# Changing the order of two jobs on VectorE and of one on ScalarE in the steady steps of a two-layer trunk

## The reference

```python
# layer 0: stick-breaking
logits = einsum(q, k) * scale
log_keep = where(strict, log_sigmoid(logits) - logits, 0)
between = cumsum(log_keep, reverse=True) - log_keep
weights = where(strict, exp(log_sigmoid(logits) + between), 0);  out = weights @ v
# layer 1: differential
probs = softmax(q @ k * scale + alibi_bias)          # two maps
weights = probs[0] - lam * probs[1];                 out = rms_norm(weights @ v) * (1 - lam_init)
# both
y = (out * silu(z)) @ w_out;   x = x + gate * rms_norm(y)
```

## Time and profile before

| | |
|---|---|
| median of 3 runs | 1470.96 us (1470.79 to 1471.69) |
| the profiled execution | 1471.86 us, its span 1470.1 us |
| TensorE busy, share of the span | 94% |
| VectorE, ScalarE, GpSimd | 69%, 62%, 22% |
| mean granted clock of TensorE | 0.980 |
| stretch 115 to 640 us, steady stick pairs | TensorE 506.2 of 525 us, VectorE 434.1 (83%), ScalarE 336.2, GpSimd 149.3, granted clock 1.00 |
| stretch 640 to 745 us, last stick pair | TensorE 90.4 of 105 us, granted clock 0.93 |
| stretch 860 to 1330 us, steady differential pairs | TensorE 454.7 of 470 us, VectorE 279.2, ScalarE 326.4, GpSimd 105.8, granted clock 1.00 |
| one steady stick pair | 77.3 us (its 1024-wide scans begin at 269.65 and 347.00) |
| scans L1586 | 128, mean 1.37 us |

### The profile page before, as it was taken

How to read it: one execution, slowest core, us unless ns; L and a number is a source line. 1 busy time by engine, 2 the same in 40 slices (tenths; PEclk the granted TensorE clock), 3 DMA queues, 4 the chain that set the end, 5 groups by cost and what they waited for, 6 DMA issues and landing times. The chain is left out here.

```text
span 1470.1 us, 23466 instructions
## 1 busy us (share of the span) xinstructions
PE 1374.6 (94%) x7206; PEld 1131.8 (77%) x7206; DVE 1015.2 (69%) x1866; ACT 909.6 (62%) x1780; POOL 326.7 (22%) x255
## 2 busy tenths in 40 slices
PE   6889999999999999988999899999999999998987
PEld 3568878787878787876778678787878778786876
DVE  4557878887888787888578665656564656565654
ACT  3556656666666665676356566767576767676632
POOL 2002323232323232322100013222222212126000
PEclk8989999999999999998999999999999999999999
DMA  9111212020212121241043111001100010003113
GB/s 342 50 36 51 65 44 72 21 86 29 71 43 71 36 71 43 64 136 37 15 160 128 29 29 30 29 29 28 43 29 29 29 29 29 29 29 115 43 65 136
DMA packets 88591, 89.90 MB, mean 61 GB/s; under 512 B 3065, under 2 KB 68834, under 8 KB 88546
## 3 DMA queue, kind: packets, MB, share of 16 engines
q1 hardware_dynamic: 88256, 89.15, 19.2%
q10 hardware_dynamic: 290, 0.18, 0.1%
HBM read 80.92 MB, written 8.40 MB: 61 GB/s over the span
## 5 line engine op out<-in xcount | busy, mean ns | idle before, releaser
L666 PE MATMUL bank<-h_hi,w_hi 128*128 128x512 f32 x928 | 377.4, 407 | 4.9 <-POOL w_lo L638 4.9
L666 PE MATMUL bank<-h_hi,w_lo 128*128 128x512 f32 x928 | 373.8, 403 | 0.0
L666 PE MATMUL bank<-h_lo,w_hi 128*128 128x512 f32 x928 | 371.6, 400 | 0.0
L1724 POOL TENSOR_TENSOR sa<-sa,keep 128x128 f32<-128x128 f32 (+7 forms) x128 | 172.0, 1346 | 469.3 <-DVE keep L1586 469.3
L666 PEld LDWEIGHTS bank<-h_hi,w_hi 128*128 128x128 f32 x928 | 176.9, 191 | 33.0 <-issue 5.0
L666 PEld LDWEIGHTS bank<-h_hi,w_lo 128*128 128x128 f32 x928 | 176.1, 190 | 32.2
L666 PEld LDWEIGHTS bank<-h_lo,w_hi 128*128 128x128 f32 x928 | 176.4, 190 | 29.2
L1586 DVE TENSOR_TENSOR_SCAN keep<-keep 128x128 f32<-128x128 f32 (+7 forms) x128 | 175.4, 1371 | 16.4 <-ACT keep L1475 15.2
L638 POOL TENSOR_TENSOR w_lo<-w_raw,w_hi 128x1024 fp32r<-128x1024 f32 x30 | 72.0, 2402 | 390.6 <-ACT w_hi L632 390.6
L1474 ACT ACTIVATE sa<-bank 128x512 f32<-128x512 f32 (+2 forms) x192 | 94.4, 492 | 68.9 <-PE bank L1358 31.8
L1487 ACT ACTIVATE wt_hi<-bank 128x512 fp32r<-128x512 f32 (+2 forms) x192 | 87.6, 491 | 58.9 <-PE bank L1374 54.9
(11 more groups left out here) (252 smaller groups left out, 2993.2 us busy)
## 6 DMA issues: line engine op xcount, KB each, us to landing
w_raw<-in_w_in_dram SPq DMA_DIRECT2D x62, 512.0 KB, 4.0
ada_slice<-in_w_ada_dram SPq DMA_DIRECT2D x64, 256.0 KB, 2.7
p_ada<-in_w_ada_dram SPq DMA_DIRECT2D x8, 1024.0 KB, 13.1
wo_raw<-in_w_out_dram SPq DMA_DIRECT2D x8, 1024.0 KB, 4.8
p_x<-in_x_dram SPq DMA_DIRECT2D x8, 512.0 KB, 7.9
o_x<-in_x_dram SPq DMA_DIRECT2D x8, 512.0 KB, 4.1
x_between<-o_res SPq DMA_DIRECT2D x8, 512.0 KB, 2.9
o_x<-x_between SPq DMA_DIRECT2D x8, 512.0 KB, 4.1
```

The lines of the kernel that those rows point to most:

```text
L666: mm = nc.tensor.matmul(self.bank[half][:, :], w[:, k, :], h[:, k, half * HALF:(half + 1) * HALF], start=(i == 0), stop=(i == GROUP - 1))
L1724: nc.gpsimd.tensor_tensor(a[:, at:S], a[:, at:S], m["keep"][KEEP[t]][:, at + 1:S + 1], ALU.mult).then_inc(weighted, 1)
```

## The change

Two moves, no instruction more or less. In the stick layer VectorE issues `weights_lo` of the tile of three steps ago ahead of the step's `scan`. In the differential layer ScalarE issues `split_hi` behind everything else of its step.

```diff
@@ stick_breaking, vector engine, pair
                     for q, g in groups(p, s, first):
                         add_parts(q, g)
+                    for q, t in tiles(p, s, first):
+                        weights_lo(q, t)
                     if s < TILES:
                         scan(p, s)
-                    for q, t in tiles(p, s, first):
-                        weights_lo(q, t)
@@ differential, scalar engine, pair
                     if s < NT:
                         exponentials(p, s)
-                    if project:
-                        for kind in SPLIT_AT[s]:
-                            proj.split_hi(act, p + 1, kind)
                     if s == 1:
                         values_hi(p)
...
                     for kind, half in U_AT[s] if project else ():
                         keep_u(p + 1, kind, half)
+                    for kind in SPLIT_AT[s] if project else ():
+                        proj.split_hi(act, p + 1, kind)
```

## The result

| | before | changed |
|---|---|---|
| median | 1471.01 us (1470.79 to 1471.69) | 1435.79 us (1435.59 to 1438.92) |
| ratio | | 0.9764 [0.9753, 0.9776] |
| the profiled execution, its span | 1471.86, 1470.1 | 1435.59, 1433.8 |
| steady stick part | 532.6 | 509.9 |
| last stick pair | 101.3 | 101.2 |

A forecast was written before the change was run, and what follows sets the result against it. TensorE, busy 94% of the span, was taken as the bound, so its waits are the gain: 22.3 + 11.4 = 33.7, less 3.7, gives 30 us and a median of 1441.0; own range 1434 to 1449, 8 in 10 1434 to 1460.

The forecast's parts named there:

- Stick pairs, 22.3: Steady stick pairs: putting `wt_lo` before the scan ends TensorE's waits for it, 22.3 us saved if nothing else is late.
- three places: TensorE's waits for `wt_lo` in steps 2, 4 and 14 of a stick pair: 6.5, 10.0 and 5.8 us saved.
- what is late next: Stick pairs, step 3: the fourth projection matmul would want the next pair's `w_lo` at 267.76, a microsecond earlier.
- `w_lo` just in time at 1.20: Stick step 3: directly behind the scan, `w_lo` takes 1.20 instead of 2.10, done at about 267.6; GpSimd's weigh stretches.
- Late copies at nothing: Stick steps 4, 6, 10 and 14: ScalarE's late copies delay VectorE's scans, covered by its idle time; cost nothing.
- the slower rival: Stick pairs: VectorE, waiting for ScalarE's copies before scans, becomes the bound; 19 us lost, 11.4 saved, 1479; chance 0.09.
- Last pair at 0: Last stick pair: TensorE waits 2.76 us, held by ScalarE's queue, so the swap gains 0, bounds -2 to +2.
- Differential pairs, 11.4: Differential pairs: moving ScalarE's `w_hi` copies last in steps 3, 6 and 8 saves 11.4 us, bounds 0 to 18.7.
- Step 3: Differential pairs: `wt_hi` of tile 1 comes 1.05 earlier, VectorE loses its 0.82 idle, shortening TensorE's `biased` wait; 5.7 us.
- Step 6: Differential pairs: `sub_sq` and `sub_o` come one copy earlier, ending TensorE's longer `sub_o` wait; 0.5 x 7 = 3.6 us.
- Step 8: Differential pairs: ScalarE's queue runs 0.3 earlier to `wt_hi` of tile 7, ending TensorE's `wt_lo` wait; 2.1 us.
- The tenth, -3.7: Whole kernel: a tenth of the 33.7 us sum, 3.7, taken off for small new waits, leaving 30.

The follow-up runs named there:

- e3_swap_three: The kernel before, with the stick swap only in steps 2, 3 and 13 of all pairs but the last; 1458.56 us, ratio 0.992.
- e12_long_gap: The changed kernel plus 32 one-column VectorE memsets between the scan and `w_lo` in step 2 of stick pairs 1 to 6; 1447.52 us, ratio 0.9841.
- e4_swap_rest: The kernel before, with the stick swap everywhere, last pair included, except in steps 2, 3 and 13 of the steady pairs; 1473.10 us, ratio 1.0016.

## Why the prediction was right

The forecast was 1441.0, the time is 1435.8: the sign, the mechanism and the range hold. Of the 5.2 us between them 3.7 are a deduction that wasn't due; the rest is 0.9 more in the two steady parts and small differences that no term held.

- **Stick pairs, 22.3.** The steady part gave 22.6. The three waits went, and the added 0.17 to 0.2 a wait for modelled ends fits: the waits sum to 18.8, the part is 22.6 shorter.
- **What the argument missed.** It gave the 22.3 to three places. `e3_swap_three` shows that they give 12.4 by themselves and that a fourth, step 14, carries the other 10, by a wait that comes up once the others are gone: by the rows some 0.46 a pair since `values` had only 0.44 to spare, and 0.90 since the scan of step 14 meets a weigh when step 13 alone is swapped. The sum was right since the change swaps every step, which the argument had not asked for: in this it was lucky. The list of what is late next went through `w_lo` and stopped before the following `values`.
- **`w_lo` just in time at 1.20.** Confirmed, 28 of 28. `e12_long_gap` puts the price at 10.6 us had GpSimd begun first at this one place of a pair. VectorE's head start was 0.16 us each time, the same as in pair 0.
- **Late copies at nothing.** Confirmed by `e4_swap_rest` in the steady pairs. VectorE's idle time before `wt_lo` (`wt_hi` not there) rose; that before `add_parts` fell, from 39.7 us to 31.3 over a like stretch. In the changed kernel TensorE never stands still in the steady stick pairs, so no late copy can have held it: the slower rival fell with its own condition.
- **Last pair at 0.** 101.2 against 101.3 us, though its waits moved from `wt_lo` to `v`.
- **Differential pairs, 11.4.** They gave 12.0. Step 3: 6.7 where 5.7 stood, in part since the wait for `biased` fell by 0.91 a time, to 0.46, and not by 0.82. Step 6: 3.5, a difference and not a run of its own, where 3.6 stood. Step 8: 1.8 where 2.1 stood.
- **The tenth, -3.7.** The mis-sized term: no new wait appeared, so what it stood for measured 0. The bare sum, 33.7, gives 1437.3.
- **What no term held.** 1.7 of the differential part's 13.7 us was the lower clock in the first 7.4 us of the kernel before, 1.3 came back in the last differential pair, whose granted clock over its 79.4 us is 0.96 instead of 0.98, and the start was 1.1 shorter, which is within its spread. Such stretches come and go between profiled executions; a difference of 1 to 2 us between two traces needs the clock beside it.

Of what would have shown it wrong, one sign came (last in this paragraph), the others were absent: no L666 waits for `w_lo` in the steady pairs. The pair period is 73.8 us, forecast as 74.2, and `biased` waits 0.46, forecast as 0.55. `sub_o` makes TensorE wait only twice in all, forecast as once a pair: the shorter wait, in step 4, was said to stay and mostly went too. VectorE's idle time before `wt_lo`, listed among the signs of being wrong, did rise, from 7.3 us over the whole kernel to 24.2, without holding TensorE.

## What to carry to other kernels

When two jobs of one engine share a step, put the one that TensorE waits for first, if the other has three steps of slack. Then look for the next wait behind the one removed, and change all steps alike or look at what a mixed order puts side by side: the swap in three steps gave 12 us where four gave 23. Price an engine's waits with the overlap of the matmuls added. Where a VectorE instruction with both inputs in SBUF meets one of GpSimd, the order in which they begin decided here which of them ran slow: put the needed instruction directly behind the one that releases the other.

## What was unexpected of the hardware

- An instruction of VectorE directly behind the scan began 0.16 us before GpSimd's, which the same scan releases, 28 times of 28. With GpSimd first at six of them the kernel's stick part was 10.6 us longer.
- A scan that is given one tile as both inputs and as output is slowed by GpSimd too: 384 columns took 2.41 instead of 0.95 us, 128 columns 1.01 in the mean instead of 0.41.
- Idle time before the first projection matmuls cost more than itself: over the same 10 us the granted clock was 0.66 with a wait of 4.86 us, 0.83 with 2.23 and 1.00 with 0.81, the last two in one trace each.
